# First layer's output projection as seven block products, its sums on VectorE, and one weight block loaded from another queue

## The chip, the cores and the metric

The kernel runs on one core of one Trainium2 chip. The metric is the device time of one execution, in microseconds (us); lower is better. The kernel before takes 2165.26 us (median of three runs, 2165.17 to 2165.53).

The engines are named as in the profile: PE is TensorE (matrix products, transpositions), PEld its weight loads, DVE is VectorE, ACT is ScalarE, POOL is GpSimd, SP is SyncE, which only issues DMAs here. Each engine runs its own instructions in order and waits for the others by semaphores.

## The reference

Two decoder layers over 1024 positions of width 1024, all in float32. The part that matters here is the output projection of layer 0, the line with `w_out`:

```python
for i in range(DEPTH):                                   # DEPTH = 2
    mk, mv = jnp.split(mem @ w_mem_kv[i], 2, axis=-1)
    if i % 2 == 0:
        h = x @ a_w_in[j]
        q, k, v, qm = jnp.split(h, [DIL_WIDTH, 2 * DIL_WIDTH, 3 * DIL_WIDTH], axis=-1)
        mix = dilated_attention(q, k, v)                 # 12 heads of 64: 768 columns
    else:
        ...                                              # gated mixer, 768 columns
    mo = memory_attention(qm, mk, mv)                    # 4 heads of 64: 256 columns
    y = jnp.concatenate([mix, mo], axis=-1) @ w_out[i]   # 1024x1024 by 1024x1024
    x = layer_norm(DN_ALPHA * x + y, ln_mix_g[i], ln_mix_b[i])
    f = (jax.nn.silu(x @ w_gate[i]) * (x @ w_up[i])) @ w_down[i]
    x = layer_norm(DN_ALPHA * x + f, ln_ffn_g[i], ln_ffn_b[i])
```

## The kernel before

**Numbers in two parts.** Every float32 operand of a product is split into a high part (rounded by the engine to the matmul's input format) and a low part (the rest). `three` (L365) makes one product of two operands as three matmuls of 128 rows by 512 columns: high by high, low by high, high by low (L367 to L369). Such a group of three is called a *piece* here. A high part is a copy, a low part a subtraction. POOL does both for weights (`split`, L324 and L327, 128x1024 each); SP loads weight block u into one of two `raw` buffers as soon as block u - 2 has been split (`load`, L249).

**Attention of layer 0.** A list of items is walked through, two heads at a time; `attention_pe`, `attention_act` and `attention_dve` hold the same list. Of each item PE makes the scores (L709, L710), transposes the probabilities (L722) and multiplies by the values (L750, L751); DVE and ACT work in between. `mix_dve` (L1013) writes the finished columns of a pair of heads, transposed (128 channels by 256 positions at a time); `mixed` counts these writes: 28 when all but the last pair are there, 32 when all are. The last pair goes to `mixL`.

**The output projection of layer 0** is a plain product. The transposed attention output (eight blocks of 128 channels) is `XTh`/`XTl`; POOL splits seven of the eight blocks (`mix_pool`, L2945 and L2948), in the order `MIX_ORDER`, mixed with the splits of the weight blocks 24 to 31; ACT and DVE split the last (L3111, L3210). PE sums in three parts of 3, 3 and 2 channel blocks over 8 position tiles and 2 column halves: 8 x 16 = 128 pieces. The first 15 stand between the items of attention (`BEFORE_SCORES`, `BESIDE`, counted from the list's end), to give PE work while it would wait. DVE adds each sum to the residual `XR` (L1122, L1125), then come the statistics, the normalisation and the transpositions for the feed-forward part (FFN; `row_turn`, L1157).

**Layer 1** already makes its output projection as seven block products (`seven_pe`, `seven_sums_dve`); its sums are at L2309 and L2333, its low parts at L2369.

**The start.** SP loads weight blocks 0 and 1, ACT's queue loads the identity, the memory rows (`memraw`) and `x`. PE's first work is to transpose `memraw` (L1069).

## Time and profile before

| | |
|---|---|
| median of three runs | 2165.26 us |
| the profiled execution | 2165.6 us, span 2163.9 us from first to last instruction |
| PE busy | 2132.7 us, 99% of the span |
| DVE, ACT, POOL busy | 62%, 44%, 60% |
| mean granted TensorE clock | 0.998 |
| first instruction of PE | at 8.12 us |
| first piece of the output projection of layer 0 | at 429.94 us |
| last write of attention (`mixed` 32) | ends at 464.62 us |
| first transposition for the FFN | at 535.4 us |

All times inside a profile count from the span's start. A row of a timeline reads: start, duration, engine, line, operation, what it writes <- what it reads, shapes, count; in brackets the idle time of the engine before it, and what ended it. Matmuls overlap, so their pace is the distance between starts, not the duration printed. Between the end of the span and the time of the execution lie 1.7 us.

### The profile page before, as it was taken

How to read it: one execution, taken by the hardware profiler on the slowest of the kernel's cores; microseconds unless marked ns; L12 is line 12 of the kernel's file. 1: busy time of each engine (PE TensorE's matmuls, PEld its weight loads, DVE VectorE, ACT ScalarE, POOL GpSimd, SP SyncE). 2: the span in 40 equal slices, each digit the busy share in tenths (PEclk: the TensorE clock that was granted, in tenths of full speed). 3: DMA queues.
4: the chain of work that ended last, by engine and by line, in shares of the span. 5: the costliest groups of instructions: out<-in, count | busy, mean ns of one | idle time of the engine just before them, and what ended most of it. 6: DMA issues, size and time to landing. Idle time of an engine off the chain costs nothing.

```text
span 2163.9 us, 32185 instructions
## 1 busy us (share of the span) xinstructions
PE 2132.7 (99%) x10912; PEld 1815.5 (84%) x10912; DVE 1352.1 (62%) x2441; ACT 954.3 (44%) x1781; POOL 1289.5 (60%) x857
## 2 busy tenths in 40 slices
PE   8999999999999999999999999999999999999997
PEld 7888888888887888888888899988878888888885
DVE  5655655655875555655557746786965655555567
ACT  5655555632544344333334754344443433343323
POOL 5221222374498777777772694504698777777764
PEclk9999999999999999999999999999999999999999
DMA  5221111141012111111131313101022111112111
GB/s 177 69 59 45 53 56 59 45 137 59 20 59 59 49 58 52 50 45 57 59 88 49 93 45 98 69 13 47 20 64 69 50 57 53 58 58 58 57 60 79
DMA packets 165726, 132.64 MB, mean 61 GB/s; under 512 B 12657, under 2 KB 148465, under 8 KB 165617
## 3 DMA queue, kind: packets, MB, share of 16 engines
q1 hardware_dynamic: 150592, 115.36, 17.5%
q10 hardware_dynamic: 15024, 15.83, 2.5%
q8 instruction: 68, 1.11, 0.2%
q14 instruction: 42, 0.34, 0.1%
HBM read 122.78 MB, written 4.19 MB: 59 GB/s over the span
## 4 chain that ended last, share of the span: by engine, by line
PE 91%; DVE 4%; POOL 3%; issue 1%; ACT 1%; DMA 0%; ACTq 0%; DVEq 0%; POOLq 0%
PE ps L367 27%; PE ps L369 27%; PE ps L368 26%; PE ps L722 3%; PE ps L750 2%; PE ps L751 2%; PE ps L709 2%; PE ps L710 2%; POOL Rl L1905 1%; PE ps L1157 1%; POOL XR L1341 1%; PE ps L1069 1%; DVE V L2708 1%; POOL raw L1927 0%; DVE T2l L1615 0%
## 5 line engine op out<-in xcount | busy, mean ns | idle before, releaser
L2111 DVE TENSOR_TENSOR XR<-XR,ps 128x512 f32<-128x512 f32 x504 | 338.5, 686 | 214.7 <-PE ps L369 214.7
L324 POOL TENSOR_TENSOR Wh<-raw,zcol 128x1024 fp32r<-128x1024 f32 x68 | 129.0, 1898 | 453.7 <-PE ps L369 376.3
L1905 POOL TENSOR_TENSOR Rl<-raw,Rh 128x512 fp32r<-128x512 f32 x216 | 285.8, 1324 | 122.1 <-ACT Rh L1749 120.1
L367 PE MATMUL ps<-XTh,Wh 128*128 128x512 f32 x608 | 248.9, 409 | 0.5 <-DVE bQl L928 0.4
L369 PE MATMUL ps<-XTh,Wl 128*128 128x512 f32 x608 | 238.4, 392 | 0.0
L368 PE MATMUL ps<-XTl,Wh 128*128 128x512 f32 x608 | 238.0, 391 | 0.0
L367 PE MATMUL ps<-XTh,Rh 128*128 128x512 f32 x576 | 224.5, 390 | 3.3 <-POOL Rl L1905 3.3
L368 PE MATMUL ps<-XTl,Rh 128*128 128x512 f32 x576 | 224.3, 389 | 0.0
L369 PE MATMUL ps<-XTh,Rl 128*128 128x512 f32 x576 | 224.3, 389 | 0.0
L1749 ACT ACTIVATE Rh<-raw 128x512 fp32r<-128x512 f32 x216 | 135.8, 630 | 167.7 <-PE ps L369 143.8
L367 PE MATMUL ps<-Wh,XTh 128*128 128x256 f32 (+1 forms) x560 | 185.9, 332 | 0.0
L369 PE MATMUL ps<-Wh,XTl 128*128 128x256 f32 (+1 forms) x560 | 184.3, 329 | 0.0
L368 PE MATMUL ps<-Wl,XTh 128*128 128x256 f32 (+1 forms) x560 | 184.2, 329 | 0.0
L1950 POOL TENSOR_TENSOR DRl<-rows,DRh 128x512 fp32r<-128x512 f32 x108 | 140.4, 1302 | 72.7 <-ACT DRh L1820 72.7
L327 POOL TENSOR_TENSOR Wl<-raw,Wh 128x1024 fp32r<-128x1024 f32 x68 | 164.2, 2414 | 5.3
L1820 ACT ACTIVATE DRh<-rows 128x512 fp32r<-128x512 f32 x108 | 68.1, 631 | 174.1 <-PE ps L369 174.1
L369 PEld LDWEIGHTS ps<-XTh,Wl 128*128 128x128 f32 x608 | 114.2, 188 | 25.5
L367 PEld LDWEIGHTS ps<-XTh,Rh 128*128 128x128 f32 x576 | 108.2, 188 | 26.5 <-POOL Rl L1905 4.2
L367 PEld LDWEIGHTS ps<-XTh,Wh 128*128 128x128 f32 x608 | 114.6, 188 | 16.4 <-issue 0.6
L368 PEld LDWEIGHTS ps<-XTl,Wh 128*128 128x128 f32 x608 | 114.9, 189 | 15.1
L369 PEld LDWEIGHTS ps<-XTh,Rl 128*128 128x128 f32 x576 | 108.2, 188 | 22.4
L368 PEld LDWEIGHTS ps<-XTl,Rh 128*128 128x128 f32 x576 | 108.2, 188 | 22.3
(325 smaller groups left out, 5628.7 us busy)
## 6 DMA issues: line engine op xcount, KB each, us to landing
raw<-in_w_up SPq DMA_DIRECT2D x44, 512.0 KB, 3.8
raw<-in_w_gate SPq DMA_DIRECT2D x72, 256.0 KB, 2.9
rows<-in_w_down SPq DMA_DIRECT2D x36, 512.0 KB, 3.6
raw<-in_a_w_in SPq DMA_DIRECT2D x20, 512.0 KB, 3.8
raw<-in_b_w_in SPq DMA_DIRECT2D x15, 512.0 KB, 3.8
B<-in_c_bias SPq DMA_DIRECT2D x12, 512.0 KB, 3.6
...
```

Source lines behind the costliest of these rows:

```text
L324: nc.gpsimd.tensor_tensor(high, raw[:, turn, :], zcol[:, 0:1].to_broadcast([P, UNIT]), ALU.add).then_inc(high_done, 1)
L327: nc.gpsimd.tensor_tensor(low, raw[:, turn, :], high.bitcast(F32), ALU.subtract).then_inc(split_done, 1)
L367: nc.tensor.matmul(dst, wh, xh, start=first, stop=False, skip_group_check=onto)
L368: nc.tensor.matmul(dst, wh, xl, start=False, stop=False, skip_group_check=onto)
L369: return nc.tensor.matmul(dst, wl, xh, start=False, stop=last, skip_group_check=onto)
L709: nc.tensor.matmul(bank(u % SU, nb), bf.Qh[:, hd, qt * P:(qt + 1) * P], K, start=True, stop=False)
L722: mm = nc.tensor.transpose(bank(4 + gi % 2, P, x * P), probs_of(g, 2 * s + ab, (lo + k) * P, (lo + k + 1) * P), ident[:, :])
L1749: nc.scalar.activation(Rh[(w - 1) % 4][:, :], source(w), ACT.Copy).then_inc(g("high"), 1)
L1820: nc.scalar.activation(DRh[:, (d - 1) % 2, :], right_source(d), ACT.Copy).then_inc(g("right_high"), 1)
L1905: nc.gpsimd.tensor_tensor(Rl[(w - 1) % 4][:, :], source(w), Rh[(w - 1) % 4][:, :].bitcast(F32), ALU.subtract).then_inc(gs[L]("low"), 1)
L1950: nc.gpsimd.tensor_tensor(DRl[:, (d - 1) % 2, :], right_source(d), DRh[:, (d - 1) % 2, :].bitcast(F32), ALU.subtract).then_inc(gs[L]("righ ...
L2111: nc.vector.tensor_tensor(x, x, bank(4 + i), ALU.add).then_inc(gf[L]("added"), 1)
```

## The change

With A the attention output (rows: positions) and B the weights, both cut into 2x2 blocks of 512, seven products of blocks take the place of eight: A11 B11, A12 B21, S4 B22, S2 T2, S3 T3, S1 T1 and A22 T4, where

- S3 = A11 - A21, S1 = A21 + A22, S2 = A22 - S3, S4 = A12 - S2 (four channel blocks each),
- T3 = B22 - B12, T2 = B11 + T3, T1 = B22 - T2, T4 = B21 - T2 (two buffers of 128x1024 each).

Each product is 4 position tiles by 4 channel blocks = 16 pieces, 112 in all. PE takes them in the order 0, 1, 6, 2, 3, 5, 4 (`ORDER0`). The results are added to `XR` by DVE (36 adds of 128x512). All of S3 and three of the four S1 are made by POOL, S2, S4 and the last S1 by DVE, right after attention, before anything else of the stage; T3(0) and T4 by POOL, the rest by DVE. Of the high parts ACT makes twenty in the stage (`first_act`) and three more before the end of attention (`ROW_HIGHS`). Weight blocks of this projection come in six units (24 to 29) and six direct loads; all later unit numbers are lower by two, and the slots differ. At the start of the kernel, weight block 1 is loaded by ACT's queue, after the first two parts of `x`, where SP's queue did it.

```diff
-U_FFN = (32, 65)
+U_FFN = (30, 63)
...
-    BEFORE_SCORES = {-15: [(0, 0)]}
-    BESIDE = {-12: [(1, 0), (0, 1), (1, 1)], -9: [(0, 2)], -6: [(1, 2), (2, 0), (2, 1)], -4: [(2, 2)], -3: [(3, 0)],
-              -2: [(3, 1)], -1: [(3, 2)]}
+    BEFORE_SCORES = {-15: [(2, 0)]}
+    BESIDE = {-12: [(3, 0), (2, 1), (3, 1)], -9: [(2, 2)], -6: [(3, 2), (0, 0), (2, 3)], -4: [(3, 3)], -3: [(1, 0)],
+              -2: [(0, 1)], -1: [(1, 1)]}
+    ROW_HIGHS = {-16: 4, -14: 6, -13: 7}
...
             if L == 0 and j == len(seq) + RECIP_AT - 1:
-                out_pe(pe, 0, (2,), range(1, 2))
+                first_piece_pe(pe, 0, 1, 3)
+                first_piece_pe(pe, 1, 0, 0)
+                first_piece_pe(pe, 1, 1, 0)
...
+    def first_piece_pe(pe, d, i, q):        # product d, position tile i, channel block q
+        c, j = q // 2, q % 2
+        r, h = PLACE0[d]
+        k = head_of(r, c, j)
+        if d == 0:
+            pe.wait_ge(*low0(0, c))
+            pe.wait_ge(*low0("A", k))
+            if i < 2 and q == 0:
+                pe.wait_ge(*at_("logits", 16 * 8))
+        elif d == 1:
+            pe.wait_ge(*low0(1, c))
+            pe.wait_ge(*low0("R", k))
...
+        before = {6: 1, 2: 0, 3: 2, 5: 6, 4: 3}.get(d)
+        if before is not None and q == 0:
+            pe.wait_ge(*go[0]("added", first_count(before, i)))
+    def first_pe(pe):
+        for i, q in [(2, 0), (3, 0)] + [(i, q) for q in (1, 3, 2) for i in range(4)]:
+            first_piece_pe(pe, 1, i, q)
...
+    def sum0_by(eng, unit, n, j):
...
+        elif n == "S1":
+            eng.wait_ge(*sum0("S3", j))
+            eng.wait_ge(*(at_("mixed", 4 * (NMP + 5)) if j == 0 else at_("mixed", 32) if j == 2 else at_("mixed", 4 * NMP)))
...
+    def first_early_pool(pool, u):
+        if u == U_OUT:
+            for j in range(4):
+                sum0_by(pool, nc.gpsimd, "S3", j)
+            for j in (1, 3):
+                sum0_by(pool, nc.gpsimd, "S1", j)
+        elif u == U_OUT + 1:
+            sum0_by(pool, nc.gpsimd, "S1", 0)
+        elif u == U_OUT + 2:
+            pool.wait_ge(*at_("v_proj", KV[8]))
+            for k in range(4):
+                high_low0_pool(pool, "A", k)
+    def first_pool(pool):
+        for k in (4, 6, 7):
+            low0_by(pool, nc.gpsimd, "R", k)
+        high_low0_pool(pool, "S4", 0)
+        high_low0_pool(pool, "S4", 3)
+        sum0_by(pool, nc.gpsimd, "T3", 0)
+        pool.wait_ge(*low0(5, 1))
...
+    def first_act(act):
+        for n, c in [("R", 5), (1, 1), (6, 0), (6, 1), ("S4", 2), ("S2", 0), ("S2", 2), ("S2", 3), (2, 0), (2, 1),
+                     ("S3", 0), ("S3", 1), (3, 0), (3, 1), ("S1", 0), ("S1", 1), (5, 0), (5, 1), (4, 0), (4, 1)]:
+            high0_act(act, n, c)
+    def first_sums_dve(dve):
+        for j in (0, 1, 3):
+            for n in ("S2", "S4"):
+                add(n, j)
+        low("R", 5)
+        low(1, 1)
+        for n in ("S1", "S2", "S4"):
+            add(n, 2)
+        first_dve(dve, 0, range(2))
+        low("S4", 2)
+        low(6, 0)
+        first_dve(dve, 1, range(1))
+        low(6, 1)
+        first_dve(dve, 1, range(1, 4))
...
         for u in range(U_OUT + 3):
+            first_early_pool(pool, u)
+            split(pool, u)
+        first_pool(pool)
...
                 for j in range(3):
-                    load(sp, 3 * p + j, src[letters(p)[j]])
+                    if (p, j) == (0, 1):
+                        load.turn += 1
+                    else:
+                        load(sp, 3 * p + j, src[letters(p)[j]])
...
         for i in range(X_PARTS):
+            if i == 2:
+                act.dma_start(raw[:, 1, :].rearrange("p (k c) -> p k c", c=P), cols(a["a_w_in"][0], 3 * DIL_W)
+                              ).then_inc(raw_landed[1], 16)
```

The order on POOL towards the end of attention. `raw`/`Wh`/`Wl` are a weight block and its parts, `mixT` the attention output; of before:

```order
L324 TENSOR_TENSOR Wh<-raw,zcol 128x1024 [waits att_q_proj,raw_landed0]
L327 TENSOR_TENSOR Wl<-raw,Wh 128x1024 [waits high_done]
L324 TENSOR_TENSOR Wh<-raw,zcol 128x1024 [waits att_k_proj,raw_landed1]
L327 TENSOR_TENSOR Wl<-raw,Wh 128x1024 [waits high_done]
L2945 TENSOR_TENSOR XTh<-mixT,zcol 128x1024 [waits att_mixed,att_v_proj]
L2948 TENSOR_TENSOR XTl<-mixT,XTh 128x1024 [waits mix_high]
```

and of the change, at the same place (`mixS` is S3, L2434 a sum; the sum between the weight blocks is S1(0)):

```order
L2434 TENSOR_TENSOR mixS_69<-mixT 128x512 [waits att_mixed] x4
L2434 TENSOR_TENSOR mixT<-mixT,mixK 128x512 [waits att_mixed,seven_right_sum] x2
L325 TENSOR_TENSOR Wh<-raw,zcol 128x1024 [waits att_q_proj,raw_landed0]
L328 TENSOR_TENSOR Wl<-raw,Wh 128x1024 [waits high_done]
L2434 TENSOR_TENSOR mixT<-mixT,mixK 128x512 [waits att_mixed,seven_right_sum]
L325 TENSOR_TENSOR Wh<-raw,zcol 128x1024 [waits att_k_proj,raw_landed1]
L328 TENSOR_TENSOR Wl<-raw,Wh 128x1024 [waits high_done]
L2461 TENSOR_TENSOR XTh<-mixT,zcol 128x512 [waits att_v_proj]
L2396 TENSOR_TENSOR XTl<-mixT,XTh 128x512 [waits mix_high]
```

Between blocks 24 and 25 stands a sum that waits for `mixed` 28; block 25 and the first split of the attention output, which the first piece reads, now stand behind it.

The order on DVE right behind the last write of attention. Of before (L1122 adds a sum of PE to the residual):

```order
L1013 TENSOR_TENSOR mixL<-ps,Os 128x256 [waits att_rden_turned,att_summed]
L1122 SCALAR_TENSOR_TENSOR XR<-XR,ps 128x512 [waits out_product] x2
L3210 TENSOR_TENSOR XTl<-mixL,XTh 128x1024 [waits last_high]
L1122 SCALAR_TENSOR_TENSOR XR<-XR,ps 128x512 [waits out_product,landed1]
```

and of the change (`mixK` and `mixL` hold the sums S2 and S4 in place; L2396 a low part, the one into `Wl` that of weight unit 27):

```order
L2434 TENSOR_TENSOR mixK<-mixK 128x512 [waits seven_sum]
L2396 TENSOR_TENSOR XTl<-mixL,XTh 128x1024 [waits seven_high]
L2396 TENSOR_TENSOR Wl<-raw,Wh 128x1024 [waits high_done]
L2434 TENSOR_TENSOR mixT<-mixT,mixL 128x512 [waits att_mixed,seven_right_sum]
L2434 TENSOR_TENSOR mixL<-mixL,mixS_69 128x512 [waits seven_low,seven_sum]
L2434 TENSOR_TENSOR mixL<-mixL 128x512 [waits seven_sum]
L2305 SCALAR_TENSOR_TENSOR XR<-XR,ps 128x512 [waits landed0,out_product] x2
L2396 TENSOR_TENSOR XTl<-mixL,XTh 128x512 [waits seven_high]
L2396 TENSOR_TENSOR Wl<-B_70,Wh 128x1024 [waits seven_high]
L2308 TENSOR_TENSOR XR<-XR,ps 128x512 [waits out_added,out_product]
```

The first row here is the last of six sums (S2 and S4 in turn, for blocks 0, 1 and 3). Before, two adds and one low part stood there; now six sums, two low parts and three more sums come ahead of the next add.

## Rows read from the trace of the kernel before

**Rows 1.** The page: busy time by engine, and the chain that ended last.

```profile
PE 2132.7 (99%) x10912; PEld 1815.5 (84%) x10912; DVE 1352.1 (62%) x2441; ACT 954.3 (44%) x1781; POOL 1289.5 (60%) x857
...
PE 91%; DVE 4%; POOL 3%; issue 1%; ACT 1%; DMA 0%; ACTq 0%; DVEq 0%; POOLq 0%
```

**Rows 2.** Busy us in 420 to 440: PE, PEld, DVE, ACT, POOL; clock.

```profile
420.00:440.00 20.00, 18.87 (x117) 15.70 (x116) 14.89 (x45) 14.37 (x34) 15.52 (x8) 1.00 0.17 52
```

**Rows 3.** Timeline of PE, 428 to 431: start, duration, what.

```profile
429.82 0.28 PE L751 MATMUL ps<-PTl,aVs 128*128 128x256 f32 x1
429.94 0.40 PE L367 MATMUL ps<-Wh,XTh 128*128 128x512 f32 x1
```

**Rows 4.** Timeline of PE in the projection, 470 to 490.

```profile
470.11 0.39 PE L367 MATMUL ps<-Wh,XTh 128*128 128x512 f32 x1
...
489.15 0.39 PE L367 MATMUL ps<-Wh,XTh 128*128 128x512 f32 x1
```

**Rows 5.** Timeline of POOL, 405 to 440.

```profile
414.98 1.89 POOL L324 TENSOR_TENSOR Wh<-raw,zcol 128x1024 fp32r<-128x1024 f32 x1 [5.21 <-PE ps L369]
...
424.16 1.90 POOL L2945 TENSOR_TENSOR XTh<-mixT,zcol 128x1024 fp32r<-128x1024 f32 x1 [4.81 <-PE ps L369]
...
432.79 1.89 POOL L324 TENSOR_TENSOR Wh<-raw,zcol 128x1024 fp32r<-128x1024 f32 x1
434.76 2.39 POOL L327 TENSOR_TENSOR Wl<-raw,Wh 128x1024 fp32r<-128x1024 f32 x1
```

**Rows 6.** Timeline of DVE: the 28th and the 32nd write of `mixed`.

```profile
426.14 0.41 DVE L1013 TENSOR_TENSOR mixT<-ps,Os 128x256 f32<-128x256 f32 x1
...
464.20 0.42 DVE L1013 TENSOR_TENSOR mixL<-ps,Os 128x256 f32<-128x256 f32 x1 [0.69 <-PE ps L760]
```

**Rows 7.** Timelines of PE, ACT, POOL and DVE at the end of attention.

```profile
463.72 0.38 PE L760 MATMUL ps<-ident,RB 128*128 128x128 f32 x2
...
464.66 1.06 ACT L3111 ACTIVATE XTh<-mixL 128x1024 fp32r<-128x1024 f32 x1 [2.04 <-DVE mixL L1013]
...
464.77 1.89 POOL L324 TENSOR_TENSOR Wh<-raw,zcol 128x1024 fp32r<-128x1024 f32 x1 [10.34 <-DVE mixL L1013]
466.74 3.27 POOL L327 TENSOR_TENSOR Wl<-raw,Wh 128x1024 fp32r<-128x1024 f32 x1
...
465.76 1.99 DVE L3210 TENSOR_TENSOR XTl<-mixL,XTh 128x1024 fp32r<-128x1024 f32 x1
```

**Rows 8.** Timeline of DVE in layer 1: sums of 128x512 and 128x1024.

```profile
1419.33 0.69 DVE L2309 TENSOR_TENSOR V<-V 128x512 f32<-128x512 f32 x1
1419.93 0.42 DVE L2747 TENSOR_TENSOR XTl<-ps,XTh 128x256 fp32r<-128x256 f32 x1
...
1428.06 1.22 DVE L2333 TENSOR_TENSOR V<-V,MO 128x1024 f32<-128x1024 f32 x1
1429.19 1.22 DVE L2333 TENSOR_TENSOR V<-V 128x1024 f32<-128x1024 f32 x1
```

**Rows 9.** Timeline of POOL: a sum of 128x512.

```profile
603.33 1.29 POOL L1927 TENSOR_TENSOR raw<-raw 128x512 f32<-128x512 f32 x1
```

**Rows 10.** Waits of PE, whole span: us in total, times, longest.

```profile
PE ps L709 <- DVE mneg L977: 1.2, 3, 0.4
```

**Rows 11.** Timelines of PE and POOL at the start.

```profile
8.12 3.65 PE L1069 MATMUL ps<-ident,memraw 128*128 128x128 f32 x16 [8.12 <-DMA memraw<-in_mem]
...
17.31 2.79 PE L1069 MATMUL ps<-ident,XR 128*128 128x128 f32 x24
...
12.07 1.89 POOL L324 TENSOR_TENSOR Wh<-raw,zcol 128x1024 fp32r<-128x1024 f32 x1 [2.02 <-DMA raw<-in_a_w_in]
```

**Rows 12.** PE's last matmul, then windows as in rows 2.

```profile
2149.10 0.39 PE L369 MATMUL ps<-Wh,hidl 128*128 128x512 f32 x1
...
2153.00:2154.00 1.00, 0.00 (x0) 0.00 (x0) 0.93 (x3) 0.21 (x1) 1.00 (x1) 1.00 0.99 406
2154.00:2155.00 1.00, 0.00 (x0) 0.00 (x0) 0.60 (x4) 0.39 (x2) 0.37 (x1) 0.51 0.19 74
```

More of the change, by code:

```diff
@@ L1158, in row_turn @@
         mm.then_inc(g("row_turned"), 1)
-    def norm_pe_after(pe, g, c):
-        def after(t):
-            for j in {5: range(4), 7: (4, 5)}.get(t, ()):
-                row_turn(pe, g, j, c)
-        return after
     def xt_unit(x, j):
@@ new lines, in build @@
+    SUMS0 = [(n, j) for j in (0, 1, 3) for n in ("S2", "S4")] + [(n, 2) for n in ("S1", "S2", "S4")] + [("T2", 0), ("T3", 1), ("T2", 1), ("T1", 0), ("T1", 1)]
+    POOL_SUMS0 = ([("S3", j) for j in range(4)] + [("S1", 1), ("S1", 3), ("S1", 0)]
+                  + [("T3", 0), ("T4", 0), ("T4", 1)])
+    g0 = Names("seven")
+    g7 = Names("seven", {"high": len(HIGHS0), "low": len(LOWS0), "sum": len(SUMS0), "right_sum": len(POOL_SUMS0),
+                         "right_low": 2}, 1)
+    ORDER0 = (0, 1, 6, 2, 3, 5, 4)
@@ new lines, in left_lows0 @@
+    def left_lows0(d, c):
+        n = LEFT0[d]
+        if n in ("S1", "S3"):
+            return [low0(n, c)]
+        return [low0(n, 0)] if c == 0 else [low0(n, 2), low0(n, 3)]
+    def first_piece_pe(pe, d, i, q):
[10 more added lines that the diff above has]
+            pe.wait_ge(*low0("R", k))
+            if i >= 2 and q == 0:
+                pe.wait_ge(*at_("mixed", 32))
+        elif j == 0:
+            pe.wait_ge(*low0(d, c))
+            for low in left_lows0(d, c) if d in LEFT0 else [low0("R", 7), low0("R", 5)]:
+                pe.wait_ge(*low)
+        before = {6: 1, 2: 0, 3: 2, 5: 6, 4: 3}.get(d)
+        if before is not None and q == 0:
+            pe.wait_ge(*go[0]("added", first_count(before, i)))
+        ts = slice(h * 512 + i * P, h * 512 + i * P + P)
+        rh, rl = (w[:, SLOT0[d] + c, j * 512:j * 512 + 512] for w in (Wh, Wl))
+        opens = d in (0, 1, 6, 5)
+        last = q == (2 if d == 1 else 3)
+        mm = three(bank(first_bank(d, i)), XTh[:, k, ts], XTl[:, k, ts], rh, rl, opens and q == 0, last, onto=not opens)
+        if last:
+            mm.then_inc(go[0]("product"), 1)
@@ new lines, in first_sums_dve, with low, add @@
+    def first_sums_dve(dve):
+        def low(n, c):
+            low0_by(dve, nc.vector, n, c)
+        def add(n, j):
+            sum0_by(dve, nc.vector, n, j)
+        for j in (0, 1, 3):
[11 more added lines that the diff above has]
+        first_dve(dve, 1, range(1, 4))
+        low("S2", 0)
+        add("T2", 0)
+        add("T3", 1)
+        low(2, 0)
+        add("T2", 1)
+        low("S2", 2)
+        low("S2", 3)
+        low(2, 1)
+        first_dve(dve, 6)
+        for n in ("S3", 3):
+            for c in range(2):
+                low(n, c)
+        first_dve(dve, 2, range(2))
+        for c in range(2):
+            low("S1", c)
+        first_dve(dve, 2, range(2, 4))
+        for c in range(2):
+            add("T1", c)
+        first_dve(dve, 3, range(1))
+        for c in range(2):
+            low(5, c)
+        first_dve(dve, 3, range(1, 4))
+        for t in range(4):
+            stats_dve(dve, go[0], None, t, range(1))
@@ L3067, in _ @@
             if L == 0:
[L3068 to L3069 removed]
+                first_pe(pe)
             else:
```

461 lines of the change are left out of this document (308 added, 153 removed).

## The prediction

> **What bounds the kernel now.** I read the page's first part and its chain first. PE is busy for 2132.7 of 2163.9 us and makes 91% of the chain [rows 1]: the kernel ends when PE's stream of products ends, and a change is worth the PE work it takes away less the PE idle time it adds. Then I read the end of attention by a window and by timelines. In 420 to 440 PE is busy for 18.87 of 20 us, beside DVE with 14.89, ACT with 14.37 and POOL with 15.52 [rows 2]: the list of items is paced by PE, with some play elsewhere. From the last reciprocal's transposition at 463.72 on, PE does nothing but pieces. The first matmuls of two pieces stand at 470.11 and 489.15, 84 matmuls apart [rows 4], so one takes 19.04 / 84 = 0.2267 us and a piece 0.68, at a granted clock of 1.00. No other engine is late there; the adds of DVE wait for PE. Last, I followed on POOL, DVE and ACT what the new stream would ask of them [rows 5 to 9].
>
> **The work removed.** 128 pieces become 112: 16 x 3 x 0.2267 = **-10.9 us**, all on the path. As many pieces as before (15) stand ahead of the last reciprocal, so the rest shrinks from 113 to 97.
>
> **First wait, before the first piece (+4.6).** Before, that piece starts at 429.94, right behind PE's work on the item ahead [rows 3], its data long there: block 25's high part started on POOL at 414.98 and the attention block's at 424.16 [rows 5]. Now POOL's row is S1(0), block 25, then block 0 of A, and S1(0) waits for `mixed` 28, which DVE gives at 426.14 + 0.41 = 426.55 [rows 6]. A sum of 128x512 takes POOL 1.29 [rows 9]: 427.84. A weight block takes 434.76 - 432.79 = 1.97 for the high part and 2.39 for the low [rows 5]: 432.20. The high part of 128x512 stands in no row; it lies between half of 1.89 and the 1.29 of a sum of this size. I take 0.95, since a sum reads two tensors and this reads one. The low part, two tensors, takes 1.29. So `mix_low` comes at 434.5, and PE idles for 434.5 - 429.9 = 4.6 (4.5 to 5.0). Behind the waiting piece on PE stand the next item's scores (L709) and the rest of attention, so nothing fills the hole, and with PE at 18.87 of 20 it isn't caught up later. What it gives back is the small waits of scores for `mneg`, 1.2 in the whole span, three of them [rows 10]: **-0.4** for the one or two that fall behind it.
>
> **Three high parts on ACT (+1.0).** Each takes 1.06 by the nearest row, L3111 [rows 7]; POOL is rid of them. The first falls beside the wait just told. The other two, 2.1 us, stand among items in which ACT has 5.6 of 20 us free. Both ends: 0 where they find that time, 2.1 plus a late exponential (1.06) where they stand ahead of work that PE needs. I take half of the 2.1, since ACT is not the bound but each row of its queue is in order.
>
> **Second wait, for the low part of unit 27 (+6.0).** `mixed` 32 comes at E = 464.20 + 0.42 = 464.62 [rows 6]. PE has nine pieces behind the last reciprocal (463.94): 6.1, so until E + 5.4. The tenth reads `Wl` of unit 27, which DVE makes behind six sums and one low part. What such a sum costs is the question. In layer 1, with POOL still, the distance between starts is 0.60 for 128x512 and 1.13 for 128x1024 [rows 8]. At the end of attention the one DVE operation with two SBUF inputs, L3210, started at 465.76 while POOL's L324 ran until 466.66, and it took 1.99; POOL's L327, started at 466.74, took 3.27 in place of 2.39 and ran on from about DVE's end at 467.75 [rows 7, 5]. Each waited for the other's end, rather than both getting slower. That has a rule in the Trainium skill, SBUF — State Buffer, section SBUF: two separate sides: a DVE operation with two SBUF inputs and a GpSimd operation share a port pair that the one who starts first holds for its whole instruction. By that rule, the trace agrees. From the two rows I let the two engines take turns. From E: S2(0), S4(0), S2(1), S4(1), S2(3) at 0.6 each and their waits, until 3.2; POOL's high part of S4(0) and S4(1) together (128x1024), which waits for S4(1) and then for its turn, 3.2 to 5.1 (1.89); DVE S4(3) to 5.7; POOL's low part of the same (2.39) to 8.1; DVE's low part of block 5 (1.14) to 9.3; POOL's high part of S4(3) (128x512, 0.95) to 10.2; DVE's low part of unit 27 to 11.4. PE idles for 11.4 - 5.4 = **6.0**. Behind its wait stand only pieces. Bounds: without turns DVE is through at 6 x 0.65 + 2 x 1.14 = 6.2, a wait of 0.8; with one more POOL row of 2.39 ahead it is 8.4.
>
> **Third wait, for the adds before product 6 (+3.7).** PE's first piece of product 6 waits for DVE's fifth to eighth `added`. Behind unit 27 stand on DVE S1(2), S2(2), S4(2), two adds, two low parts and the next add; on POOL the low part of S4(3) and T3(0), a sum of 128x1024 (2.39 by L327's row). In turns: POOL low to 12.7 (1.29 and the change-over of 1.1 counted from 11.4), DVE S1(2) to 13.3, POOL T3(0) to 15.6, DVE S2(2) and S4(2) to 17.0, adds at 0.6 to 18.2, low parts to 19.9, add to 20.5. PE's eight pieces, started at E + 11.4, end at 16.8: 20.5 - 16.8 = **3.7**. Bounds: 0 without turns, 5 if low parts of the right-hand blocks take POOL's 2.39 in their way once more.
>
> After that the products need 10.9 us each and DVE's share of one is four to six adds, two sums and two low parts, some 7 us: I see no further wait until the row turn, where before 535.4 stood.
>
> **The start (-0.4).** PE starts at 8.12, released by `memraw`, and block 1 lands in `raw` at about 12.07 [rows 11]. With block 1 behind part of `x` on ACT's queue, `memraw` shares the DMA engines with one block less. Both ends: 0.2 (a single packet's turn) and 1.1, if all of block 1's share ahead of 8.12 went to it. I take 0.4: both blocks and `memraw` share one saturated set of engines, and block 1's split comes later in exchange, which is off PE's path until the memory keys are due.
>
> **The sum.** -10.9 + 4.6 - 0.4 + 1.0 + 6.0 + 3.7 - 0.4 = +3.6. The profiled execution took 2165.6 (span 2163.9 + 1.7), 0.3 above the median: **2169.2 us**, 2166 to 2172.5 by the bounds that go with port turns. A run can be told from no change here by 0.2%, 4.3 us: faster is under 2160.9, slower over 2169.6.
>
> **Rivals.**
> *The sums are cheap.* If DVE's sums run as in layer 1 whatever POOL does, the second wait is 0.8 and the third 0: -10.9 + 4.6 - 0.4 + 1.0 + 0.8 - 0.4 = -5.3, **2160.3**. For it: layer 1 makes the same sums at 0.60 [rows 8]. Against it: POOL stood still beside them, and where it did not the row is 1.99 [rows 7].
> *The clock falls (slower side).* The two waits of 4.6 and 6.0 fall in a stretch in which PE never rests now. After PE's last matmul (2149.10 + 0.39) the granted clock stands at 1.00 in 2153 to 2154 and 0.51 in 2154 to 2155 [rows 12], that is at 1.2 GHz, about 4.5 us after PE stopped. So either wait may just reach it. Price: at the start 16 transpositions take 3.65, 0.23 each, and the next 24 at 17.31 take 2.79, 0.116 each [rows 11]; the slow stretch 8.12 to 14.6 does in 6.5 us what 3.7 would do, 2.8 lost. Behind the second wait PE's slowness is mostly paid by the third; behind the first it isn't: +2.8, **2172.0**, and 2173 to 2175 where both are paid. [...] TensorE: Matmul & The Clock Gate of the Trainium skill, section Part 1: The HAM clock gate, says likewise that an idle array falls back to 1.2 GHz; no row here shows it in mid-kernel.
> *A new wait at the FFN's head.* POOL makes T4's sums and low parts (four rows, 9.6) and then splits four blocks in a row (4 x 4.3 = 17.2), where the splits stood spread out before. If the last of these is late for the first FFN product, PE waits up to 3: **2170 to 2172**. Against it: 26.8 us of POOL work against three products, 32.7.
> *Larger gains at the head and in attention:* start -1.1, ACT's rows free, unit 27 a turn earlier (-2.4): **2165**.
>
> **How the numbers follow.** Forecast 0.38; clock 0.25; cheap sums 0.15; late FFN 0.10; larger gains 0.12. Within the forecast's own range a good half lies under 2169.6, as do the larger gains. Faster: most of the cheap sums, 0.13. Slower: a bit under half of the forecast (0.17), the clock (0.21) and the late FFN (0.06): 0.44. Same: 0.43. Range 2160.5 to 2174.5: it holds the cheap sums' place at its lower edge and the clock's case with one wait.
>
> **What would show it.** Right: PE's first piece at about 434.5, after a wait of 4.6 ended by POOL's low part of 128x512; between E + 3 and E + 16, DVE's sums of 128x512 at 1.5 to 2.8 us each instead of 0.6, and POOL's low part of S4(0) over 2.39; PE waits of 6 for the low part of unit 27 and of 3.7 for an add to `XR`; the first transposition for the FFN at 535.4 + 4; PE's first instruction at 7.7. Wrong: sums of 0.6 beside a busy POOL (the cheap case); a granted clock of 0.5 behind 434 or 476 (the clock); a PE wait on `Wh` or `Wl` at the FFN's head.

## The result, and the profile after

The changed kernel takes **2170.44 us** (median of 12 runs, 2169.73 to 2172.54), the kernel before 2165.27: 5.2 us slower, ratio 1.0025, 95% interval 1.0017 to 1.0032. The forecast was 2169.2, in a range of 2160.5 to 2174.5. The profiled execution took 2172.54 (span 2170.8), 2.1 above the median; a second profile of the same program, further down, is the typical one.

The page of the change: busy time by engine, and the chain [rows 1].

```profile
PE 2128.4 (98%) x10864; PEld 1809.8 (83%) x10864; DVE 1380.4 (64%) x2456; ACT 975.2 (45%) x1803; POOL 1285.0 (59%) x860
...
PE 89%; DVE 4%; POOL 3%; issue 1%; ACT 1%; DMA 1%; SPq 0%; ACTq 0%; DVEq 0%; POOLq 0%
```

48 matmuls are gone, and PE is busy 4.3 us less and not 10.9. Most of the other 6.6 are products that ran at half speed: in the three slow stretches below PE is busy for some 11.9 us, half of which, 5.9, the slow clock adds. What PE waited for in 400 to 560: us in total, times, longest.

```profile
PE ps L368 <- POOL XTl L2396: 4.6, 1, 4.6
PE ps L368 <- DVE Wl L2396: 3.7, 1, 3.7
PE ps L762 <- DVE Os L1009: 3.2, 2, 2.3
PE ps L368 <- DVE XR L2308: 1.8, 1, 1.8
```

The first, second and fourth are the three waits of the forecast. The third wasn't in it. The same end of attention on PE's timeline (L762 is L760 of before):

```profile
6.62 3.65 PE L1073 MATMUL ps<-ident,memraw 128*128 128x128 f32 x16 [6.62 <-DMA memraw<-in_mem]
...
428.44 0.28 PE L753 MATMUL ps<-PTl,aVs 128*128 128x256 f32 x1
433.36 0.77 PE L368 MATMUL ps<-Wh,XTh 128*128 128x512 f32 x1 [4.65 <-POOL XTl L2396]
...
445.39 0.41 PE L762 MATMUL ps<-ident,RB 128*128 128x128 f32 x2 [0.94 <-DVE Os L1009]
...
472.12 0.41 PE L762 MATMUL ps<-ident,RB 128*128 128x128 f32 x2 [2.27 <-DVE Os L1009]
...
483.96 0.79 PE L368 MATMUL ps<-Wh,XTh 128*128 128x512 f32 x1 [3.67 <-DVE Wl L2396]
...
492.78 0.47 PE L368 MATMUL ps<-Wh,XTh 128*128 128x512 f32 x1 [1.76 <-DVE XR L2308]
...
541.87 1.91 PE L1165 MATMUL ps<-ident,XR 128*128 128x128 f32 x16
```

PE starts 1.5 us earlier than in [rows 11]. The first piece stands at 433.36 and not at 429.94 [rows 3], the last reciprocal's transposition at 472.12 and not at 463.72 [rows 7]. POOL ahead of the first piece, beside [rows 5]:

```profile
425.31 1.29 POOL L2434 TENSOR_TENSOR mixT<-mixT,mixK 128x512 f32<-128x512 f32 x1 [16.92 <-DVE mixK L1023]
426.55 1.90 POOL L325 TENSOR_TENSOR Wh<-raw,zcol 128x1024 fp32r<-128x1024 f32 x1
...
430.84 1.04 POOL L2461 TENSOR_TENSOR XTh<-mixT,zcol 128x512 fp32r<-128x512 f32 x1
431.95 1.26 POOL L2396 TENSOR_TENSOR XTl<-mixT,XTh 128x512 fp32r<-128x512 f32 x1
```

POOL stood for 16.92 us in front of one sum, with block 25 landed behind it. And the clock (columns as in rows 2: PE, PEld, DVE, ACT, POOL, then the granted clock):

```profile
431.00:432.00 1.00, 0.00 (x0) 0.00 (x0) 0.00 (x0) 0.00 (x0) 0.92 (x2) 1.00 0.30 14
432.00:433.00 1.00, 0.00 (x0) 0.00 (x0) 0.00 (x0) 0.00 (x0) 1.00 (x1) 0.60 0.66 186
...
438.00:439.00 1.00, 1.00 (x5) 0.85 (x4) 0.10 (x2) 1.00 (x3) 0.93 (x1) 0.50 0.00 0
```

PE had stood still since 428.7; from 432.2 to 439.0 the clock is at 0.50 (1.2 GHz), and from 433.4 on PE is busy again. The same happens twice more, in 473.2 to 476.6 and 483.4 to 486.8. Last, DVE and then POOL behind the end of attention (E = 473.05 here):

```profile
475.62 0.68 DVE L2434 TENSOR_TENSOR mixK<-mixK,mixS 128x512 f32<-128x512 f32 x1
476.34 2.27 DVE L2434 TENSOR_TENSOR mixK<-mixK 128x512 f32<-128x512 f32 x1
478.53 3.39 DVE L2396 TENSOR_TENSOR XTl<-mixL,XTh 128x1024 fp32r<-128x1024 f32 x1
481.85 2.06 DVE L2396 TENSOR_TENSOR Wl<-raw,Wh 128x1024 fp32r<-128x1024 f32 x1
```

```profile
475.85 2.21 POOL L2461 TENSOR_TENSOR XTh<-mixK,zcol 128x1024 fp32r<-128x1024 f32 x1 [24.19 <-DVE mixK L2434]
478.14 2.71 POOL L2396 TENSOR_TENSOR XTl<-mixK,XTh 128x1024 fp32r<-128x1024 f32 x1
480.81 2.02 POOL L2461 TENSOR_TENSOR XTh<-mixK,zcol 128x512 fp32r<-128x512 f32 x1
```

Read them as one column: DVE's sum ends at 476.30, POOL's row ends at 478.06, DVE's sixth sum at 478.61, POOL's low part at 480.85, DVE's low part at 481.92, POOL at 482.83, DVE at 483.91. Each row's end is about its own bare length (0.6 or 1.2 on DVE; 1.9, 2.4, 1.0 on POOL) behind the other's. Unit 27 is ready at E + 10.9 (11.4 was forecast), product 6 starts at E + 19.7 (20.5).

### The profile page after: what moved, and what is told of

The parts are those of the page before. It is cut to its first block, busy times and chain, and to the rows that moved or that the text cites. A ratio compares the mean times of both kernels' runs of the same rounds, so it can differ in the third digit from the quotient of the medians.

```text
span 2170.8 us, 32242 instructions
## 1 busy us (share of the span) xinstructions
PE 2128.4 (98%) x10864; PEld 1809.8 (83%) x10864; DVE 1380.4 (64%) x2456; ACT 975.2 (45%) x1803; POOL 1285.0 (59%) x860
## 4 chain that ended last, share of the span: by engine, by line
PE 89%; DVE 4%; POOL 3%; issue 1%; ACT 1%; DMA 1%; SPq 0%; ACTq 0%; DVEq 0%; POOLq 0%
PE ps L368 26%; PE ps L370 26%; PE ps L369 26%; PE ps L724 3%; PE ps L711 2%; PE ps L712 2%; PE ps L752 1%; PE ps L753 1%; POOL Rl L1887 1%; POOL XR L1323 1%; PE ps L1165 1%; PE ps L1073 1%; DVE V L3028 1%; DMA XR<-in_x 1%; POOL raw L1909 0%
## 5 line engine op out<-in xcount | busy, mean ns | idle before, releaser
L325 POOL TENSOR_TENSOR Wh<-raw,zcol 128x1024 fp32r<-128x1024 f32 x63 | 119.7, 1900 | 404.5 <-PE ps L370 337.7
L370 PE MATMUL ps<-XTh,Wl 128*128 128x512 f32 x608 | 238.3, 392 | 0.0
L370 PE MATMUL ps<-XTh,Rl 128*128 128x512 f32 x576 | 224.1, 389 | 0.0
L368 PE MATMUL ps<-Wh,XTh 128*128 128x256 f32 (+1 forms) x544 | 181.2, 333 | 10.1 <-POOL XTl L2396 4.6
L369 PE MATMUL ps<-Wl,XTh 128*128 128x256 f32 (+1 forms) x544 | 179.2, 329 | 0.0
L370 PE MATMUL ps<-Wh,XTl 128*128 128x256 f32 (+1 forms) x544 | 179.1, 329 | 0.0
L328 POOL TENSOR_TENSOR Wl<-raw,Wh 128x1024 fp32r<-128x1024 f32 x63 | 151.3, 2402 | 4.9
L370 PEld LDWEIGHTS ps<-XTh,Wl 128*128 128x128 f32 x608 | 114.1, 188 | 25.6
L880 ACT ACTIVATE PTh<-ps 128x512 fp32r<-128x512 f32 (+1 forms) x152 | 85.2, 564 | 96.5 <-PE ps L724 85.8
L370 PEld LDWEIGHTS ps<-XTh,Rl 128*128 128x128 f32 x576 | 108.1, 188 | 22.5
```

Source lines behind the costliest of these rows:

```text
L325: nc.gpsimd.tensor_tensor(high, raw[:, turn, :], zcol[:, 0:1].to_broadcast([P, UNIT]), ALU.add).then_inc(high_done, 1)
L328: nc.gpsimd.tensor_tensor(low, raw[:, turn, :], high.bitcast(F32), ALU.subtract).then_inc(split_done, 1)
L368: nc.tensor.matmul(dst, wh, xh, start=first, stop=False, skip_group_check=onto)
L369: nc.tensor.matmul(dst, wh, xl, start=False, stop=False, skip_group_check=onto)
L370: return nc.tensor.matmul(dst, wl, xh, start=False, stop=last, skip_group_check=onto)
L880: nc.scalar.activation(PTh[:, b:b + n, :], bank(4 + gi % 2, n * P).rearrange("p (k q) -> p k q", q=P), ACT.Copy).then_inc(at_("pt_high"), 1)
```

## The experiments

The changed kernel's median is 2170.44, and 2170.67 in its second set of runs; differences below are given from both. "Before" is 2165.14 to 2165.36 in all sets.

**The start alone.** The kernel before, with only the load of block 1 moved:

```diff
-                    load(sp, 3 * p + j, src[letters(p)[j]])
+                    if (p, j) == (0, 1):
+                        load.turn += 1
+                    else:
+                        load(sp, 3 * p + j, src[letters(p)[j]])
...
         for i in range(X_PARTS):
+            if i == 2:
+                act.dma_start(raw[:, 1, :].rearrange("p (k c) -> p k c", c=P), cols(a["a_w_in"][0], 3 * DIL_W)
+                              ).then_inc(raw_landed[1], 16)
```

> The kernel before, with only the start changed: weight block 1 on ScalarE's queue behind two parts of x. The trace of the change shows PE's first instruction at 6.62 us where before it stood at 8.12. Theory 1: the earlier memory rows are worth the whole 1.5 us to the end, so 2163.8 and PE's first instruction near 6.6. Theory 2 (the prediction's): they are worth 0.4, the rest is given back at the later landing of block 1, so 2164.9. Theory 3: the 1.5 at the start came from the run and not from the order of loads: 2165.3 and PE's first instruction near 8.1.

2164.11 us (2163.72 to 2164.40), 1.1 below the kernel before; in the profile PE starts at 6.80 and the first row turn stands at 533.91, 1.5 earlier than before. Theory 1, a little smaller in the median than in the profile; theories 2 and 3 fall. The bytes say where the time comes from: until PE's first instruction the DMA engines moved 1.93 MB before (238 GB/s over 8.12 us) and 1.56 MB here (230 over 6.80). The 0.37 MB less are most of block 1; at 385 GB/s they are about 1.0 us by this estimate. The rest fits the rate in 4 to 6 us, 400 GB/s here and 343 before.

**S1(0) behind the splits of A11.**

```diff
-        elif u == U_OUT + 1:
-            sum0_by(pool, nc.gpsimd, "S1", 0)
         elif u == U_OUT + 2:
             pool.wait_ge(*at_("v_proj", KV[8]))
             for k in range(4):
                 high_low0_pool(pool, "A", k)
+            sum0_by(pool, nc.gpsimd, "S1", 0)
```

> The changed kernel, with one sum moved on POOL: S1(0), which waits for write 28 of attention, stands behind the four splits of A11 and no longer ahead of weight block 25. Theory 1: the first wait and the fall of the clock behind it both come from this sum. PE then waits under 0.5 us before the first piece (4.65 in the changed kernel), the granted clock stays at 1.00 in 430 to 440, and the time falls by 4.2 + 1.9 = 6 to 2164.3. Theory 2: the clock does not fall because of this wait; the time falls by 4.2 to 2166.2 and the clock still falls near 433. Theory 3: the lead is lost in a later wait (the residual's loads, the sums on VectorE), since those hang on other things; the time falls by under 2.

2164.59 us, 5.9 to 6.1 below the change. The first piece now stands right behind PE's work, without a wait:

```profile
428.48 0.40 PE L368 MATMUL ps<-Wh,XTh 128*128 128x512 f32 x1
```

The clock is at 1.00 through 428 to 442. Theory 1; all of it stays to the end, so the later waits move along with the end of attention. (The profiled run took 2166.37, the slowest of eleven. In it PE waits 2.18 before the last reciprocal's transposition, as in the first profile of the change, and the clock falls behind that; the row of DVE that holds it up stood 2.76 us for the DMA of x.)

**PE kept at work through the first wait.**

```diff
+                        pe.wait_ge(*low0(0, 0))
+                        for _ in range(19):
+                            nc.tensor.matmul(bank(2), Wh[:, 0, 0:P], Wh[:, 0, 0:512], start=True, stop=True)
                         first_piece_pe(pe, 0, i4, k)
```

> The changed kernel, with 19 products of 128x512 whose result nobody reads, put on PE ahead of its first piece, where it waits for 4.65 us. The wait for POOL stays as long as it was. Theory 1: the clock falls because PE stands still. The filling takes 19 x 0.227 = 4.3 us, PE's wait shrinks to some 0.3, the granted clock stays at 1.00 in 432 to 439, and the time falls by what the slow stretch costs, 1.9: 2168.5. Theory 2: the slow stretch is no cost of its own, because the items behind it wait for ACT and DVE anyway: the time stays at 2170.4.

PE's timeline, and two windows of it:

```profile
428.44 4.50 PE L783 MATMUL ps<-Wh 128*128 128x512 f32 x19
433.32 0.47 PE L368 MATMUL ps<-Wh,XTh 128*128 128x512 f32 x1 [0.39 <-POOL XTl L2399]
```

```profile
432.00:434.00 2.00, 1.61 (x8) 1.05 (x7) 0.00 (x0) 0.00 (x0) 2.00 (x2) 1.00 0.71 250
434.00:436.00 2.00, 1.75 (x13) 1.41 (x11) 0.91 (x2) 0.49 (x1) 1.92 (x3) 1.00 0.00 1
```

The piece starts where it did, the clock stays up, and the time is 2169.54: 0.9 to 1.1 less. The clock's fall is a cost of its own, but only about half of the 1.9 expected. Two things make it smaller. In the second profile of the change, which is next, the slow stretch ends at 437.5 and not at 439, and between the same marks of PE (the first piece, and the transpositions at 436.59 before and 441.05 after) it costs 1.3. And with the clock up, a wait of scores for `mneg` is back, 0.40 at 436.15, which the slow stretch had hidden.

**The change once more**, with no edit.

> The changed kernel once more, for a second profile of it. Its first profiled execution took 2172.54 where the median of its runs was 2170.44. Theory 1: the wait before the last reciprocal's transposition (2.27) varies with the landing of the residual's loads, and the second fall of the clock, behind it, does not come in every run. A typical run has that wait at 0.8 to 1.2 and two falls of the clock instead of three, and takes 2170.4. Theory 2: three falls are the rule, and the profile of 2172.5 differs by something later in the program.

2170.67 us, the profiled run 2170.25. PE's timeline of it:

```profile
444.74 0.41 PE L762 MATMUL ps<-ident,RB 128*128 128x128 f32 x2 [1.13 <-DVE Os L1009]
...
469.81 0.41 PE L762 MATMUL ps<-ident,RB 128*128 128x128 f32 x2 [0.55 <-DVE Os L1009]
...
481.63 0.80 PE L368 MATMUL ps<-Wh,XTh 128*128 128x512 f32 x1 [5.25 <-DVE Wl L2396]
...
490.44 0.47 PE L368 MATMUL ps<-Wh,XTh 128*128 128x512 f32 x1 [1.35 <-DVE XR L2308]
```

Theory 1. The wait before the last reciprocal is 0.55 here and 2.27 in the first profile, and behind it the clock doesn't fall: it is down in 430 to 438 and 478 to 486 only. With E = 470.75, product 6 starts at E + 19.7, as in the first profile, though the waits are 5.25 and 1.35 there and 3.67 and 1.76 here. The split between the two waits depends on how fast PE came to them; their end doesn't.

**x ahead of B22 on SP's queue.**

```diff
-            sp.wait_ge(*at_("logits", 16 * 8))
-            both(B22, "22", "landed4")
             for i in range(4):
...
                 if i == 2:
+                    sp.wait_ge(*at_("logits", 16 * 8))
+                    both(B22, "22", "landed4")
                     sp.wait_ge(*at_("mixed", 32))
```

> The changed kernel with one move on SP's queue: the first two loads of x into the residual go ahead of the two loads of B22, as they go ahead of all late weight blocks in the kernel before. Theory 1: VectorE's first two adds at the end of attention wait for these loads, and with them the last reciprocal (1.2 to 2.3 us of PE's wait, and the clock's second fall where it comes). Then DVE's adds wait for nothing, that PE wait falls to the 0.2 of its own chain, and the time falls by 1 to 2, to 2168.4 to 2169.4. Theory 2: VectorE's turns with POOL behind it set the time from the end of attention to product 6 anyway (19.7), but they start with attention's end, so the gain stays. Theory 3: B22 is now late for ScalarE's high parts and the third wait takes the gain back: 2170.4.

2169.92 us, 0.5 to 0.8 less, where theory 1 gave 1 to 2. DVE's adds, here and in the second profile of the change:

```profile
466.13 1.25 DVE L2305 SCALAR_TENSOR_TENSOR XR<-XR,ps 128x512 f32<-128x512 f32 x2
```

```profile
467.62 1.28 DVE L2305 SCALAR_TENSOR_TENSOR XR<-XR,ps 128x512 f32<-128x512 f32 x2 [1.13 <-DMA XR<-in_x]
```

DVE's wait is gone, and with it PE's wait before the last reciprocal's transposition. The mechanism is that of theory 1; its size is that of a typical run (a wait of 0.55) and not of the first profile (2.27). The move takes two things away: x no longer stands behind 1 MB of B22, and it no longer stands behind SP's wait for the last scores, which came with B22 (its first load is issued at 454.89 in place of 457.50). The runs don't part the two. The first profile blamed PE's L370 for DVE's wait, whose end (469.85) fell together with the landing; in the second the DMA is named.

**ScalarE's third row later.**

```diff
-    ROW_HIGHS = {-16: 4, -14: 6, -13: 7}
+    ROW_HIGHS = {-16: 4, -14: 6, -8: 7}
```

> The changed kernel with ScalarE's third high part of the attention rows (block 7) made 5 items later. Theory 1: this row holds up a high part of probabilities, with it DVE's low part and halves, and with them PE's second reciprocal transposition (a wait of 1.1 us, 0.2 before the change): that wait falls to 0.2 to 0.3 and the time by 0.9, to 2169.6. Theory 2: the wait there comes from the first wait and the slow clock ahead of it, which put the engines out of step: it stays at about 1, and so does the time at 2170.5.

2169.38 us, 1.1 to 1.3 less, and the wait before the second reciprocal's transposition is 0.26 in place of 1.13 (the stretch from 427.6 to it shrinks from 17.20 to 16.10). Theory 1; theory 2 falls a second time in the kernel with S1(0) moved, which has neither the first wait nor the slow clock and still waits 1.20 here.

**POOL held back until unit 27 is ready.**

```diff
+        pool.wait_ge(*low0(1, 1))
         high_low0_pool(pool, "S4", 0)
         high_low0_pool(pool, "S4", 3)
```

> The changed kernel, with one wait more on POOL: its splits of S4 begin only when DVE has made the low part of unit 27. Nothing is taken away. Theory 1: DVE's slow rows in that stretch (sixth sum 2.27, low parts 3.39 and 2.06) come from turns with POOL. Then the sixth sum takes 0.7, the two low parts 1.2 each, PE's second wait (3.67) goes, and the third (1.76) grows, because POOL's splits are later; the time falls by 0 to 3, to 2167.4 to 2170.4. Theory 2: these rows are slow for another reason (PE's reads, the DMA of B22 and B11 that lands there). Then they stay at 2 to 3.4 us and the time grows by the later splits, to above 2173.

DVE, then two rows of POOL, the first one held back:

```profile
474.38 0.69 DVE L2434 TENSOR_TENSOR mixK<-mixK 128x512 f32<-128x512 f32 x1
474.99 1.22 DVE L2396 TENSOR_TENSOR XTl<-mixL,XTh 128x1024 fp32r<-128x1024 f32 x1
476.13 1.21 DVE L2396 TENSOR_TENSOR Wl<-raw,Wh 128x1024 fp32r<-128x1024 f32 x1
...
477.98 2.27 DVE L2434 TENSOR_TENSOR mixL<-mixL,mixS 128x512 f32<-128x512 f32 x1
480.28 2.77 DVE L2434 TENSOR_TENSOR mixL<-mixL 128x512 f32<-128x512 f32 x1
482.97 1.27 DVE L2305 SCALAR_TENSOR_TENSOR XR<-XR,ps 128x512 f32<-128x512 f32 x2
```

```profile
477.42 2.27 POOL L2461 TENSOR_TENSOR XTh<-mixK,zcol 128x1024 fp32r<-128x1024 f32 x1 [26.02 <-DVE Wl L2396]
...
482.46 1.48 POOL L2461 TENSOR_TENSOR XTh<-mixK,zcol 128x512 fp32r<-128x512 f32 x1
```

The same three rows of DVE that took 2.27, 3.39 and 2.06 take 0.69, 1.22 and 1.21 with POOL still, and the two sums behind POOL's start take the 2.27 and 2.77 instead. That settles the turns. The second wait falls to 0.7, the third grows to 6.7, and the time rises to 2172.38. A gain of nothing to 3 was expected, and it came out as a loss of 1.7 to 1.9. Product 6 does not start later (E + 18.8, with E = 471.09), but the clock is at 0.50 behind the long third wait, until 495.8, where nothing hides it: from product 6 to the row turn PE needs 51.9 in place of 49.1.

**S4's high parts on ScalarE.**

```diff
-        high_low0_pool(pool, "S4", 0)
-        high_low0_pool(pool, "S4", 3)
+        low0_by(pool, nc.gpsimd, "S4", 0)
+        low0_by(pool, nc.gpsimd, "S4", 3)
...
-        for n, c in [("R", 5), (1, 1), (6, 0), (6, 1), ("S4", 2),
+        for n, c in [("R", 5), (1, 1), ("S4", 0), (6, 0), (6, 1), ("S4", 3), ("S4", 2),
```

> The changed kernel with the high parts of S4(0), S4(1) and S4(3) made by ScalarE (two rows, 1.1 and 0.6) and no longer by POOL (two rows, 2.2 and 2.0 with their waits). Theory 1: from the end of attention to product 6 the time is set by the rows of DVE with two SBUF inputs and POOL's rows taking turns, one after the other. Then DVE's sixth sum takes 0.7 in place of 2.3, its low part of block 5 about 2.4 or less in place of 3.4, PE's second and third wait shrink together by 2 to 3, and the time falls by 2 to 3, to 2168. Theory 2: only POOL's low parts (two inputs each) stand in DVE's way, and the high parts with their one tensor do not: then DVE's rows keep their durations and the time stays within 0.5.

2168.53 us, 1.9 to 2.1 less. DVE:

```profile
474.33 0.69 DVE L2434 TENSOR_TENSOR mixK<-mixK 128x512 f32<-128x512 f32 x1
474.94 3.42 DVE L2396 TENSOR_TENSOR XTl<-mixL,XTh 128x1024 fp32r<-128x1024 f32 x1
```

The sixth sum is at 0.69, so POOL's high part, which adds a zero column to one tensor, takes turns as well: theory 2 falls. The low part behind it, for which theory 1 gave 2.4 or less, still waits for a POOL row (its low part of S4(0), started at 474.86). PE's second wait is 3.95 and there is no third, together 2.7 less than in the second profile. The gain is at the lower end of theory 1.

**DVE's two low parts early.**

```diff
             for n in ("S2", "S4"):
                 add(n, j)
-        low("R", 5)
-        low(1, 1)
+            if j == 0:
+                low("R", 5)
+                low(1, 1)
```

> The changed kernel with one move on VectorE: its two low parts (block 5, unit 27), which PE's second wait hangs on, stand behind its second sum and no longer behind its sixth. No work is added or taken away. Theory 1: DVE's and POOL's turns are one chain of 19.7 us from the end of attention to product 6, and order within it changes little. Then the second wait (5.2) goes to under 0.5, the third grows from 1.4 by about 6 or 7 less what the clock no longer costs, product 6 starts 19 to 20 us behind the end of attention as before, and the time stays at 2170.5 within 1. Theory 2: the waits are two separate prices, as the prediction adds them up (6.0 and 3.7): then the second goes and the third stays, and the time falls by 4 to 5.

PE's only wait behind the reciprocal:

```profile
489.75 0.76 PE L368 MATMUL ps<-Wh,XTh 128*128 128x512 f32 x1 [7.33 <-DVE XR L2308]
```

The second wait (5.25) is gone, the third went from 1.35 to 7.33, product 6 starts at E + 18.4 (E = 471.35), 1.3 earlier than before, where theory 1 gave no change to speak of. The time is 2171.38, 0.7 to 0.9 more: the 1.3 us gained on the chain are given back by the clock, which is now down behind the third wait, on PE's path (from product 6 to the row turn 50.5 in place of 49.1). Theory 2, two prices that add up, falls. It is one chain, and moving a wait along it gained nothing here.

**PE kept at work through the second wait.** The filling overwrites the bank in which product 0 waits for product 2, so that one partial sum is lost; no work is left out.

```diff
+            if (i, q) == (0, 3):
+                pe.wait_ge(*go[0]("added", 1))
+                for _ in range(20):
+                    nc.tensor.matmul(bank(2), Wh[:, 2, 0:P], Wh[:, 2, 0:512], start=True, stop=True)
             first_piece_pe(pe, 1, i, q)
```

> The changed kernel with 20 products of 128x512, whose result nobody reads, put on PE ahead of the piece that waits for unit 27. Theory 1: the clock's fall behind that wait costs PE 2.0 us over eight pieces, and the third wait, set by DVE, takes it up: with the filling the granted clock stays at 1.00 from 478 to 486, the third wait grows from 1.4 to 3.4, and the time stays at 2170.5 within 0.5. Theory 2: the slow pieces are a price of their own: the time falls by 1.5 to 2.

PE's timeline and three windows:

```profile
482.60 0.50 PE L368 MATMUL ps<-Wh,XTh 128*128 128x512 f32 x1 [0.76 <-DVE Wl L2400]
...
491.45 0.76 PE L368 MATMUL ps<-Wh,XTh 128*128 128x512 f32 x1 [3.07 <-DVE XR L2312]
```

```profile
488.00:490.00 2.00, 0.38 (x2) 0.00 (x0) 2.00 (x4) 2.00 (x4) 0.00 (x0) 1.00 1.03 422
490.00:492.00 2.00, 0.55 (x1) 0.50 (x2) 2.00 (x3) 0.42 (x1) 0.00 (x0) 0.69 0.47 190
492.00:494.00 2.00, 2.00 (x6) 1.60 (x5) 2.00 (x4) 0.00 (x0) 0.00 (x0) 0.50 0.00 0
```

The clock stays up behind the second wait and the third grows from 1.35 to 3.07, as theory 1 says; product 6 starts at E + 19.8 (E = 471.68). But the time is 2172.17, 1.5 to 1.7 more and not the same: the clock is at 0.50 from 490.8 to 497.6, behind the longer third wait, where it holds up product 6 (51.9 from there to the row turn in place of 49.1). The six runs spread from 2170.51 to 2173.91 and the profiled one is the slowest, so a typical run may pay less. The slow pieces behind the second wait are hidden, and those behind the third are not. Theory 2 falls too.

**All of it together, twice.** The moves of S1(0), x, ScalarE's row, the high parts of S4 and the two low parts in one kernel, with T3(0) on VectorE, the adds ahead of the sums of block 2, and

```diff
-            for i in units:
-                for q in range(4):
-                    first_piece_pe(pe, d, i, q)
+            for i, q in ([(i, q) for qs in ((0, 1), (2, 3)) for i in units for q in qs] if d == 6 else
+                         [(i, q) for i in units for q in range(4)]):
+                first_piece_pe(pe, d, i, q)
```

> All that the runs point to, in the changed kernel: S1(0) behind the splits of A11 on POOL; x ahead of B22 on SP; the high parts of S4 on ScalarE; T3(0) on VectorE; VectorE's two low parts behind its second sum, and the low part of B22 and the adds ahead of the sums of block 2; product 6 by channel pairs, so that S4(2) is read 5 us later; ScalarE's third row of attention 5 items later. Theory 1 (all waits hang on POOL, DVE's turns and the loads): first wait and clock -5.9 (measured), loads -1.2, ScalarE's row -0.7, and product 2 starts 24.5 us behind the end of attention in place of 30.6, -6: 2156.5 us. Theory 2: once the head of the stage is shorter, later sums of VectorE are late for products 2 and 3, and half of that last term is lost: 2159.5. The kernel before, with its start changed alone, takes 2164.1.

2158.26 us (2157.49 to 2160.13), ratio to before 0.9971 (0.9959 to 0.9982). Between the two theories. Of the 12.2 us that this is below the change, the moves timed alone add up to some 9 to 10; what T3(0) and the new order add was not timed apart. PE waits 0.5, 1.0 and 0.9 us in the stage. The second version puts B22's low part between the sums and orders the rest anew:

```diff
-        low(6, 0)
+            if j == 1:
+                low(6, 0)
         first_dve(dve, 0, range(2))
-        first_dve(dve, 1, range(1))
+        first_dve(dve, 1, range(2))
...
-        low("S2", 0)
         add("T2", 0)
-        add("T3", 1)
+        low("S2", 0)
         low(2, 0)
+        add("T3", 1)
```

> The version of 2158.3 with its rows in another order: the low part of B22 between VectorE's sums, ahead of POOL's two low parts (ScalarE makes its high part first); two adds of product 1 ahead of the sums of block 2; T2(0) and the low part of T2 ahead of T3(1); product 2 by channel pairs too. Theory 1: the three waits that PE has left in the stage (0.5, 1.0 and 0.9 us) all hang on VectorE's order, and go: 2156 us. Theory 2: one of them moves to product 3, since VectorE has as much work as before: 2157 to 2158.

2156.57 us (median of 7, from 2156.04; two of the seven took 2161.3 and 2161.9, at a mean granted clock of 0.996 where the other five have 0.998, and were not profiled), ratio to before 0.9968 (0.9957 to 0.9979), 8.6 below the kernel before and 13.9 below the change. Theory 1 in the time. PE:

```profile
462.05 0.38 PE L762 MATMUL ps<-ident,RB 128*128 128x128 f32 x2
...
474.37 0.47 PE L368 MATMUL ps<-Wh,XTh 128*128 128x512 f32 x1 [0.32 <-DVE XR L2308]
...
477.62 0.47 PE L368 MATMUL ps<-Wh,XTh 128*128 128x512 f32 x1 [0.27 <-DVE XR L2308]
...
524.32 1.91 PE L1165 MATMUL ps<-ident,XR 128*128 128x128 f32 x16
```

62.27 us lie between the first and the last of these, where before it was 71.67 (463.72 to 535.39) and in the change 69.71. The waits have not all gone: two are left, 0.6 together, both for adds to `XR`. The granted clock is 1.00 from 466 to 494. So 9.4 of the 10.9 us of the pieces taken out arrive; 0.6 of the other 1.5 are these waits, and where the rest goes was not traced.

## Why the prediction was right, point by point

The second profile of the change, against that of before, from PE's marks (the reciprocals' transpositions at 429.21, 439.36, 463.72 before and 427.54, 444.74, 469.81 after; the row turn at 535.39 and 539.52; PE's last matmul at 2149.10 and 2153.80):

| term | forecast | measured |
|---|---|---|
| start, up to the first mark | -0.4 | -1.67 |
| first wait | +4.6 | +4.66 |
| clock behind it | 0 (rival: 2.8) | +1.9, the rest of 7.05 |
| ScalarE's rows | +1.0 | +0.9 |
| small waits given back | -0.4 | -0.4 |
| loads of x | 0 | +0.7 |
| fewer pieces, second and third wait | -10.9 + 6.0 + 3.7 = -1.2 | -1.96 |
| behind the row turn | 0 | +0.6 |
| sum | +3.6 | +4.7 |

The small waits are those of scores for `mneg`: 1.2 in three before, 0.8 in two after; the one behind the first wait is gone.

**The mechanism held.** The three waits came in their places, with their releasers. The first was right to 0.1 because every row of it stood in the trace, but for the high part of 128x512 (0.95 taken, 1.04 measured). Both of its ends came 1.1 to 1.5 earlier than forecast, with the start.

**The turns between DVE and POOL held**, and they decided the sign. From the two rows of [rows 7] the forecast laid out the order by hand; it put unit 27 at E + 11.4 and product 6 at E + 20.5, and they came at 10.9 and 19.7. Of the four sums behind `mixed` 32 that it wanted at 1.5 to 2.8, three took that (2.27, 1.76 and 2.76) and the fourth 0.69. Its step of POOL's low part of S4(3), until E + 12.7, is E + 11.4 and 1.29; the change-over named beside it is not in that sum. The kernel with POOL held back shows that the turns are the cause (2.27, 3.39 and 2.06 with POOL at work, 0.69, 1.22 and 1.21 without). The Trainium skill's page SBUF — State Buffer, section SBUF: two separate sides, has a DVE operation with two SBUF inputs and a GpSimd operation that reads SBUF lock each other out for a whole instruction. The runs agree. The rival of cheap sums (2160.3) fell with it.

**Adding the second and third wait was right only as a sum.** The forecast had 6.0 and 3.7; the runs had 5.25 and 1.35, and about 1.9 of slow pieces between them (eight pieces from 481.63 to 488.9, 7.3 in place of 5.44). The chain of DVE and POOL fixes where both end. The prediction said this of the clock alone ("mostly paid by the third"), and the filling of the second wait showed it.

**The start was undersized**: -1.1 in the median and -1.5 in the profile for a term put at -0.4, with 1.1 as its outer bound. The step that failed is the choice of 0.4 between the two ends: by the bytes moved, `memraw` gained most of block 1's share ahead of PE's start, which is the outer end. The higher rate in 4 to 6 us (400 GB/s in place of 343) lies beyond that bound, and why it is higher was not tested.

**The clock's rival was half right.** It said that the clock might fall; it fell behind the first wait in every profile that had it unfilled, and behind the second or third. The forecast's own sum had the clock at nothing, so a cost that it left to a rival came in. The price at the first is 1.9 by the table, 1.5 once the small wait that it hides is taken off, and 0.9 to 1.1 by the kernel with the filling; it is not 2.8. The 2.8 came from the start's slow stretch of 6.5 us (the 32 transpositions there end at about 14.35, which gives 2.5); here PE was back at work for about 4.4 us of the slow clock (433.1 to 437.5). The prediction's one row on the fall had PE still for some 4.5 us. Here the clock fell after PE had been still for 3.5 us (428.7 to 432.2 in the first profile) and for 2.3 (428.4 to 430.7 in the second). It fell behind the wait of 2.27 as well, at 473.2, when PE was back at work for 1.1 us. The Trainium skill's TensorE: Matmul & The Clock Gate, section Part 1: The HAM clock gate, has the idle array fall back to 1.2 GHz. The trace agrees (0.50 granted, and a matmul of 128x512 at 0.427 between starts in place of 0.227).

**A queue was left out.** The prediction followed POOL, DVE, ACT and the start's queues, but not SP's at the end of attention: B22, 1 MB, and SP's wait for the last scores stand ahead of the residual's x there, and DVE's adds, which need x, stand ahead of `Os`, which the last reciprocal's transposition needs. That cost 0.7; in the run that was profiled first it cost 2.4, and the clock fell behind it. The late FFN (a rival of up to 3) came to 0.6, of which 0.36 is one wait of PE for an add to `XR` at 601.6; POOL's four splits in a row are not what PE waits for there.

The errors partly cancel: the start came out 1.3 better than forecast and the stage itself 0.8, against 1.9 of clock, 0.7 of loads and 0.6 behind the row turn. The waits were foreseen; that the sum is off by only 1.2 us is in part luck.
